# Memory's key and value projection: x's normed part and the reciprocal root in PSUM banks, and ScalarE's publication one tile later

## The chip, the cores and the metric

The kernel runs on one core of one Trainium2 chip. The metric is the device time of one launch in microseconds. Three runs of the kernel before gave 2895.95, 2902.23 and 2911.4 us; their median, 2902.23 us, is the time to beat.

## What is computed

The reference runs two blocks of two transformer layers each on x of 512 tokens by 1024 features, in float32. The change lies in the second block, in each layer's cross attention to a memory of 256 rows. Cut to that:

```
def rmsnorm(x, g):
    return x * lax.rsqrt(jnp.mean(x * x, axis=-1, keepdims=True) + EPS) * g

def second_block(x, mem, ...):
    for layer in range(2):
        y = mixer(rmsnorm(x, g_mix_pre[layer]))          # forgetting attention, then a gated recurrence
        x = x + rmsnorm(y, g_mix_post[layer])            # the x that the change touches
        h = rmsnorm(x, g_cross_pre[layer])
        m = rmsnorm(mem, g_mem[layer])
        k, v = jnp.split(m @ w_xkv[layer], 2, axis=-1)   # the key and value projection
        y = attention(h @ w_xq[layer], k, v) @ w_xo[layer]
        x = x + rmsnorm(y, g_cross_post[layer])
        ...                                              # feed forward
```

## The kernel before, in words

Everything is feature-major: x lies in SBUF as 8 parts of 128 partitions by 512 tokens, `x[:, m]`. Products of float32 are made of three matmuls (L562 to L564): a number is split into a high part in fp32r and the low rest, and TensorE adds high by high, low by high and high by low. A linear layer is a row of output tiles, each of 128 features. Tile m takes one chunk of weights, 128 x 1024, and 24 matmuls.

**The path of a chunk.** SyncE's queue loads chunk c into one of RING = 4 slots as soon as the low part of chunk c-4 is made. ScalarE makes the high part (`high`, w_hi, L1011), and waits for that slot's matmuls of chunk c-4. GpSimd makes the low part (`low`, w_lo, L484), after w_hi. TensorE's tile waits for w_lo. ScalarE stands LEAD = 3 chunks ahead: it issues w_hi of chunk m+3 at tile m.

**The stage.** `memory_attention(e)` begins with `xkv0` (and `xkv1` in the second layer): 16 tiles over memory's 256 rows, so that a matmul has 256 columns. Tiles 0 to 7 are keys (k_x), 8 to 15 are values (z_vx). VectorE evacuates each out of one of four PSUM banks (L1478); TensorE's tile m waits for the evacuation of tile m-4. Beside it the same engines finish x, since the mixer's output y_mid is still to be normed and added: after TensorE has summed the squares of y_mid (L648), `inverse_rms` makes the reciprocal root (L1454, ScalarE's root L1054, L1457) into `rstd`. Then, within VectorE's tile m for m < 8, `add_normed` multiplies y_mid by rstd in place (L1738) and adds it, times a gain, to x (L1739). ScalarE waits for that x, squares it (L1018) and makes its high part xh (L1023); that is `renormed` and `publish`. VectorE's `publish(m-1)` adds the squares up (acc, L1428) and makes the low part xl (L1435). The next layer, `xq`, multiplies xh and xl by its weights, and TensorE reads nothing of x before it.

**The order** on each engine is the program's, written out by hand. ScalarE's tile m is w_hi of chunk m+3, then `renormed(m)`. VectorE's tile m is the evacuation, L1738, L1739, then `publish(m-1)`: L1428 and L1435. ScalarE's square of part m, for m of 3 and more, waits until acc has taken in part m-2 (there are two buffers, tmpa), which is the line `act.wait_ge(acc_ready, n_.acc.n + m - 2)`.

PSUM has 8 banks. The projections use 0 to 3, bank 7 (`MISC`) holds the sums of squares, and attention uses 4 to 6 as well, at other times. `add_normed_rows` (L1759, L1763), the sister of `add_normed` behind xo and the feed forward, keeps both of these in banks already: the reciprocal root in bank 7 and the normed part in banks 4 to 6.

Of the kernel before, what the change touches and what calls it, by code (L numbers as in the profile page):

```python
# [17 lines left out]
KT = D // P  # L18
# [122 lines left out]
def two_stacks(nc, x_in, mem_in, weights, small_in, tables_in, rope_in, cmpmask_in, sel_dram, out):  # L141
    f32, f32r = mybir.dt.float32, mybir.dt.float32r
    ALU, ACT, AX = mybir.AluOpType, mybir.ActivationFunctionType, mybir.AxisListType
    ctx = ExitStack()
    with ctx:
        def sb(name, shape, dt=f32):
            return ctx.enter_context(nc.sbuf_tensor(name, shape, dt))

        def sem(name):
            return ctx.enter_context(nc.semaphore(name))  # L150


        x = sb("x", [P, KT, T])
# [5 lines left out]
        rstd = sb("rstd", [P, T])  # L159
# [28 lines left out]
        def place(name, shape, kib, dt=f32):  # L188
            if kib == 0:
                with nc.sbuf_tensor(name, shape, dt) as here:  # L190
                    return here
            with nc.sbuf_tensor(name + "_below", [P, int(kib * 256)], f32):
                with nc.sbuf_tensor(name, shape, dt) as here:
                    return here
# [53 lines left out]
        y_mid = place("y_mid", [P, KT, T], 48)  # L248
# [15 lines left out]

        ps = ctx.enter_context(nc.psum_tensor("ps", [P, 8, T], f32))
        S_BANKS, PT_BANKS, MISC = (0, 1, 2), (3, 6), 7


        w_in = [sem(f"w_in{s}") for s in range(RING)]
# [12 lines left out]
        x_ready = sem("x_ready")  # L282
# [38 lines left out]
        def gain(name, m):  # L321
            s = SMALL[f"g_{name}"].start + m
            return small[:, s:s + 1]
# [668 lines left out]
        def _(act):  # L992
            n_ = Shared()
# [26 lines left out]
            def publish(m, name):  # L1020

                square(x[:, m], m)
                A(xh[:, m], x[:, m], ACT.Copy, scale=gain(name, m)).then_inc(xh_ready, 1)  # L1023
# [28 lines left out]
            def root(n=T):  # L1052
                act.wait_ge(var_done, n_.var.next())
                A(tmpb[:, 0, 0:n], tmpb[:, 0, 0:n], ACT.Sqrt).then_inc(sd_done, 1)  # L1054

            def steps(name):
                c0 = CHUNK0[name]
                for m in range(TILES[name]):
                    if m or name not in ROWS:
                        high(c0 + m + LEAD)  # L1060
                    yield m, BANK0[name] + m
# [8 lines left out]
            def copy_values(dst, n):  # L1070
                act.wait_ge(vt_ready, n_.vt.next())
                bank = ps[:, 4 + (n_.vt.n - 1) % 4, :]
                A(dst, bank.rearrange("p (k c) -> p k c", c=dst.shape[-1]), ACT.Copy).then_inc(vt_copied, 1)
# [6 lines left out]
            def attention(steps, hooks, hi=xh):  # L1080

                s0 = n_.pairs.n
                n_.pairs.n += len(steps)
                for s in range(len(steps) + LAG):
                    slot = (s0 + s) % 4

                    def exponential(a):
                        u, n = steps[s]["two"][a], 2 * (s0 + s) + a
                        p = pr[:, n % 8, 0:u["nk"] + (u["sink"] is not None)]
                        act.wait_ge(sm_done, n + 1)  # L1090
                        A(p, p, ACT.Exp, scale=-1.0, bias=negm[:, slot, a:a + 1],  # L1091
                          accum_out=den[:, slot, a:a + 1]).then_inc(p_ready, 1)

                    def copy_turned():
                        n = 2 * (s0 + s - TURN) + 1
                        nk = steps[s - TURN]["two"][1]["nk"]
                        act.wait_ge(pt_ready, n + 1)
                        if n >= 4:
                            act.wait_ge(o_done, (n - 3) // 2)
                        A(pt[:, n % 4, 0:nk], ps[:, PT_BANKS[1], 0:nk], ACT.Copy).then_inc(pt_copied[1], 1)  # L1100

                    if s < len(steps):
                        exponential(0)
                    if TURN <= s < len(steps) + TURN:
                        copy_turned()
                    if s < len(steps):
                        exponential(1)
                    if s >= LAG and steps[s - LAG]["ends"]:
                        split_mix(steps[s - LAG]["group"], hi, s0 + s - LAG + 1)
                    for hook in hooks.get(s, []):  # L1110
                        hook()
# [158 lines left out]
            def renormed(m, name):  # L1270
                act.wait_ge(x_ready, n_.x.next())
                publish(m, name)
# [27 lines left out]
            def memory_attention(e):  # L1300
                for m, g in steps(f"xkv{e}"):
                    if m == 0:
                        root()
                    if m < KT:
                        renormed(m, f"cross_pre{e}")
                for j in range(4):
                    copy_values(v_x[:, :, j * 256:(j + 1) * 256], j)
                for m, g in steps(f"xq{e}"):
                    if m == 0:
                        root()  # L1310
                attention(UX, {})
                squares_out(f"xo{e}", y_mid)
                renormed_first(f"gu{2 + e}", f"ffn_pre{e}")
                gate_up(2 + e)
                squares_out(f"dn{2 + e}", y_dn, DN_CHUNKS)
# [93 lines left out]
        def _(dve):  # L1409
            n_ = Shared()  # L1410
            V = nc.vector
# [6 lines left out]
            def link(ins):  # L1418

                dve.wait_ge(dve_self, mark(ins))  # L1420
# [10 lines left out]
            def publish(m, name):  # L1431

                dve.wait_ge(xh_ready, n_.xh.next())
                accumulate(m)
                V.scalar_tensor_tensor(out=xl[:, m], in0=x[:, m], scalar=gain(name, m),  # L1435
                                       in1=fp(xh)[:, m], op0=ALU.mult,
                                       op1=ALU.subtract).then_inc(xl_ready, 1)
# [13 lines left out]
            def inverse_rms(dst, eps, n=T):  # L1451

                dve.wait_ge(ss_done, n_.ss.next())
                V.tensor_scalar(tmpb[:, 0, 0:n], ps[:, MISC, 0:n], 1.0 / D, eps, ALU.mult,  # L1454
                                ALU.add).then_inc(var_done, 1)
                dve.wait_ge(sd_done, n_.sd.next())
                link(V.reciprocal(dst[:, 0:n], tmpb[:, 0, 0:n]))  # L1457
# [13 lines left out]
            def tiles(name):  # L1471
                for m in range(TILES[name]):
                    dve.wait_ge(chunk_done, CHUNK0[name] + m + 1)
                    yield m, ps[:, (BANK0[name] + m) % 4, :]
# [139 lines left out]
            for m in range(17):  # L1614
                dve.wait_ge(chunk_done, in_e_chunk(m) + 1)
                bank = ps[:, (BANK0["in_e"] + m) % 4, :]
# [103 lines left out]
            def x_updated(ins):  # L1720
                ins.then_inc(x_ready, 1)
                n_.x.next()
# [10 lines left out]
            def copy_out(y):  # L1733
                return lambda m, bank: V.tensor_copy(y[:, m], bank)

            def add_normed(y, name, m):

                link(V.tensor_tensor(y[:, m], y[:, m], rstd[:], ALU.mult))  # L1738
                x_updated(V.scalar_tensor_tensor(out=x[:, m], in0=y[:, m], scalar=gain(name, m),  # L1739
                                                 in1=x[:, m], op0=ALU.mult, op1=ALU.add))  # L1740

            def copies_out(name, y, n_k=1):
# [49 lines left out]
                                           op1=ALU.subtract).then_inc(mem_ready, 1)  # L1792

            def memory_attention(e):
                for m, bank in tiles(f"xkv{e}"):
                    if m == 0:
                        inverse_rms(rstd, 1e-6)
                    scaled(k_x[:, m] if m < 8 else z_vx[:, m - 8], bank, MEM, rstd_m).then_inc(evac_done, 1)
                    if m < KT:
                        add_normed(y_mid, f"mix_post{e}", m)  # L1800
                    dve.wait_ge(evac_done, BANK0[f"xkv{e}"] + m + 1)
                    V.engine_nop().then_inc(proj_ready, 1)
                    if 1 <= m <= KT:
                        publish(m - 1, f"cross_pre{e}")
                for m, bank in tiles(f"xq{e}"):
                    if m == 0:
                        inverse_rms(rstd, 1e-6)
                    scaled(q_x[:, m], bank).then_inc(evac_done, 1)
                    dve.wait_ge(evac_done, BANK0[f"xq{e}"] + m + 1)
                    V.engine_nop().then_inc(proj_ready, 1)  # L1810
                attention(UX, {})
                copies_out(f"xo{e}", y_mid)
                inverse_rms_rows(1e-6)
                add_normed_rows(y_mid, f"cross_post{e}", f"ffn_pre{e}")
                gate_up(2 + e)
                copies_out(f"dn{2 + e}", y_dn, DN_CHUNKS)
                inverse_rms_rows(1e-6)
                add_normed_rows(y_dn, f"ffn_post{e}", None if e else "mix_pre1")
# [314 lines left out]
```

## Time and profile before

| | |
|---|---|
| median of three runs | 2902.23 us |
| profiled execution, its own time | 2906.3 us |
| its span | 2904.5 us |
| TensorE busy | 2762.4 us, 95% |
| GpSimd busy | 1280.0 us, 44% |
| ScalarE busy | 1094.4 us, 38% |
| VectorE busy | 1074.2 us, 37% |

The profiled execution took 1.8 us more than its span, and 4.1 us more than the median of the runs. The busy shares are means over the whole kernel. The stage that is changed lies twice in it: its first matmul starts at 1563.5 us in the first layer, and the same stage comes again about 762 us later. In the rows, times of start are us from the span's start.

### The profile page before, as it was taken

The numbers are of one execution on the slowest core, as the hardware profiler recorded it, in microseconds if no ns is written. First come the engines' busy times: TensorE is split into PE (matmuls) and PEld (weight loads), VectorE is DVE, ScalarE is ACT, GpSimd is POOL, SyncE is SP. The second block draws the span as 40 slices with busy tenths as digits, with TensorE's granted clock in tenths as the row PEclk, the third lists the DMA queues.
The fourth block names the chain that finished last, engine by engine and source line by source line (L and its number), as shares of the span: only waits on it lengthen the run. The fifth ranks groups of instructions, "written<-read, shape, count | busy, mean of one in ns | idle before, by whom it ended". The sixth has DMA issues, their size and how long they took to land.

```text
span 2904.5 us, 37907 instructions
## 1 busy us (share of the span) xinstructions
PE 2762.4 (95%) x13516; PEld 2255.4 (78%) x13516; DVE 1074.2 (37%) x1941; ACT 1094.4 (38%) x1777; POOL 1280.0 (44%) x715
## 2 busy tenths in 40 slices
PE   6999999999989999999998999999988889999998
PEld 5756888888857888878767887888876788788886
DVE  5675322112664222123445434221055673432212
ACT  5665323222664332232243334232236443333221
POOL 3544444444444444454324534444443363454442
PEclk9999999999999999999979999999998999999999
DMA  4301332333202223322203412323322231233331
GB/s 151 129 2 32 99 94 93 101 109 98 94 9 77 94 94 101 102 94 88 87 15 95 130 44 80 99 90 104 105 86 67 95 123 59 66 101 94 101 102 65
DMA packets 69090, 251.79 MB, mean 87 GB/s; under 512 B 7672, under 2 KB 7928, under 8 KB 68736
## 3 DMA queue, kind: packets, MB, share of 16 engines
q1 hardware_dynamic: 67104, 244.35, 26.4%
q10 hardware_dynamic: 1888, 6.14, 0.6%
q8 instruction: 61, 1.00, 0.2%
q14 instruction: 37, 0.30, 0.0%
HBM read 248.36 MB, written 2.10 MB: 86 GB/s over the span
## 4 chain that ended last, share of the span: by engine, by line
PE 88%; DVE 8%; issue 2%; ACT 2%; POOL 0%; DMA 0%; DVEq 0%; POOLq 0%; ACTq 0%
PE ps L562 26%; PE ps L563 26%; PE ps L564 26%; PE ps L700 4%; PE ps L725 3%; PE ps L711 2%; DVE acc L1428 1%; DVE xl L1435 1%; DVE pr L1528 0%; DVE y_mid L1738 0%; PE ps L670 0%; DVE ps L1759 0%; DVE r_l L1920 0%; DVE x L1739 0%; PE ps L648 0%
## 5 line engine op out<-in xcount | busy, mean ns | idle before, releaser
L484 POOL TENSOR_TENSOR w_lo<-w_raw,w_hi 128x1024 fp32r<-128x1024 f32 x462 | 1117.5, 2423 | 1357.8 <-ACT w_hi L1011 1357.5
L562 PE MATMUL ps<-xh,w_hi 128*128 128x512 f32 x2384 | 940.5, 395 | 43.6 <-DVE xl L1435 22.2
L563 PE MATMUL ps<-xl,w_hi 128*128 128x512 f32 x2384 | 933.7, 392 | 0.0
L564 PE MATMUL ps<-xh,w_lo 128*128 128x512 f32 x2384 | 933.4, 392 | 0.0
L1011 ACT ACTIVATE w_hi<-w_raw 128x1024 fp32r<-128x1024 f32 x462 | 484.4, 1053 | 548.1 <-PE ps L564 544.8
L562 PEld LDWEIGHTS ps<-xh,w_hi 128*128 128x128 f32 x2384 | 452.1, 190 | 143.6 <-issue 43.2
L563 PEld LDWEIGHTS ps<-xl,w_hi 128*128 128x128 f32 x2384 | 451.9, 190 | 94.5 <-issue 1.7
L564 PEld LDWEIGHTS ps<-xh,w_lo 128*128 128x128 f32 x2384 | 451.3, 189 | 94.6
L562 PE MATMUL ps<-hh,w_hi 128*128 128x512 f32 x704 | 273.9, 389 | 0.0
L563 PE MATMUL ps<-hl,w_hi 128*128 128x512 f32 x704 | 273.9, 389 | 0.0
L564 PE MATMUL ps<-hh,w_lo 128*128 128x512 f32 x704 | 273.9, 389 | 0.0
L1132 ACT ACTIVATE tmpa<-tmpa 128x512 f32<-128x512 f32 x88 | 55.6, 632 | 427.4 <-DVE tmpa L1478 427.3
L1478 DVE TENSOR_TENSOR tmpa<-ps,rstd 128x512 f32<-128x512 f32 x88 | 60.8, 691 | 385.6 <-PE ps L564 385.6
L1091 ACT ACTIVATE pr<-pr,negm 128x512 f32<-128x512 f32 (+2 forms) x224 | 120.0, 536 | 125.3 <-DVE negm L1528 125.1
L531 POOL TENSOR_SCALAR pr<-pr,wgt,ones 128x256 f32<-128x256 f32 (+3 forms) x160 | 91.3, 581 | 159.9 <-DVE wgt L1542 159.9
L564 PEld LDWEIGHTS ps<-hh,w_lo 128*128 128x128 f32 x704 | 132.2, 188 | 27.6
L562 PEld LDWEIGHTS ps<-hh,w_hi 128*128 128x128 f32 x704 | 132.2, 188 | 27.4
L563 PEld LDWEIGHTS ps<-hl,w_hi 128*128 128x128 f32 x704 | 132.2, 188 | 27.2
L1478 DVE TENSOR_TENSOR tmpb<-ps,rstd 128x512 f32<-128x512 f32 x96 | 66.3, 691 | 155.5 <-PE ps L564 155.4
L1588 DVE TENSOR_TENSOR x<-ps,x 128x512 f32<-128x512 f32 x32 | 22.1, 692 | 271.3 <-PE ps L564 271.3
L1528 DVE CUSTOM_DVE_ANT_0 pr<-ps,tab 128x512 f32<-128x512 f32 (+2 forms) x192 | 85.7, 477 | 85.4 <-PE ps L700 84.4
L562 PE MATMUL ps<-mem_h,w_hi 128*128 128x256 f32 x256 | 79.1, 309 | 20.3 <-POOL w_lo L484 20.3
(259 smaller groups left out, 2917.0 us busy)
## 6 DMA issues: line engine op xcount, KB each, us to landing
w_raw<-weights_in SPq DMA_DIRECT2D x462, 512.0 KB, 3.5
x<-x_in ACTq DMA_DIRECT2D x4, 512.0 KB, 10.7
mem<-mem_in ACTq DMA_DIRECT2D x2, 1024.0 KB, 4.9
x_out<-x SPq DMA_DIRECT2D x4, 512.0 KB, 2.6
rope<-rope_in ACTq DMA_DIRECT2D x1, 512.0 KB, 12.2
tab<-tables_in ACTq DMA_DIRECT2D x2, 256.0 KB, 2.9
tab<-tables_in ACTq DMA_DIRECT2D x1, 384.0 KB, 12.5
small<-small_in ACTq DMA_DIRECT2D x1, 326.5 KB, 5.4
```

The source lines that it names most:

```text
L484: nc.gpsimd.tensor_tensor(w_lo[:, slot], w_raw[:, slot], w_hi.bitcast(f32)[:, slot], ALU.subtract).then_inc(lo_ready, 1)
L531: nc.gpsimd.tensor_scalar(p, p, w, gate, ALU.mult, ALU.mult).then_inc(pn_ready, 1)
L562: nc.tensor.matmul(dst, w_hi[:, slot, w], hi, start=first, stop=False)
L563: nc.tensor.matmul(dst, w_hi[:, slot, w], lo, start=False, stop=False)
L564: return nc.tensor.matmul(dst, w_lo[:, slot, w], hi, start=False, stop=last)
L700: last = nc.tensor.matmul(ps[:, S_BANKS[n % 3], 0:u["nk"]], q, k, start=c == 0, stop=c == parts - 1)
L711: last = nc.tensor.transpose(ps[:, PT_BANKS[a], tokens(kb)], pr[:, n % 8, tokens(kb)], ident[:])
L725: last = nc.tensor.matmul(ps[rows, g["bank"], tokens(column)], values[kb], pt[:, (n + a) % 4, tokens(kb)], start=st["opens"] and kb == 0, ...
L1011: A(w_hi[:, s], w_raw[:, s], ACT.Copy).then_inc(hi_ready, 1)
L1091: A(p, p, ACT.Exp, scale=-1.0, bias=negm[:, slot, a:a + 1], accum_out=den[:, slot, a:a + 1]).then_inc(p_ready, 1)
L1478: return V.tensor_tensor(dst, bank[0:rows, 0:n], r[0:rows, 0:n], ALU.mult)
L1528: V.tensor_tensor_reduce(out=pr[:, n % 8, 0:nk], in0=ps[:, S_BANKS[n % 3], 0:nk], in1=u["mask"], scale=-u["scale"], scalar=start, op0=ALU.add,
```

## The change

It has two parts. First, VectorE writes the reciprocal root of the mixer's output into PSUM bank 6 rather than into SBUF, and the normed part of y_mid into bank 4 or 5 in turn rather than back over y_mid; L1739 reads it there. A wait keeps the bank of part m-2 until x has taken it in. Second, the publication of x's parts is moved by one tile: ScalarE does `renormed(m-1)` in tile m, for m of 1 to 8, and VectorE does `publish(m-2)` in tile m, for m of 2 to 9.

```
+        NORMED_BANKS, RSTD_BANK = (4, 5), 6
...
                 for m, g in steps(f"xkv{e}"):
                     if m == 0:
                         root()
-                    if m < KT:
-                        renormed(m, f"cross_pre{e}")
+                    if 1 <= m <= KT:
+                        renormed(m - 1, f"cross_pre{e}")
...
-            def add_normed(y, name, m):
+            def add_normed(y, name, m, x0):
 
-                link(V.tensor_tensor(y[:, m], y[:, m], rstd[:], ALU.mult))
-                x_updated(V.scalar_tensor_tensor(out=x[:, m], in0=y[:, m], scalar=gain(name, m),
+                bank = ps[:, NORMED_BANKS[m % 2], :]
+                if m >= 2:
+                    dve.wait_ge(x_ready, x0 + m - 1)
+                link(V.tensor_tensor(bank, y[:, m], ps[:, RSTD_BANK, :], ALU.mult))
+                x_updated(V.scalar_tensor_tensor(out=x[:, m], in0=bank, scalar=gain(name, m),
                                                  in1=x[:, m], op0=ALU.mult, op1=ALU.add))
...
             def memory_attention(e):
+                x0 = n_.x.n
                 for m, bank in tiles(f"xkv{e}"):
                     if m == 0:
-                        inverse_rms(rstd, 1e-6)
+                        inverse_rms(ps[:, RSTD_BANK, :], 1e-6)
                     scaled(k_x[:, m] if m < 8 else z_vx[:, m - 8], bank, MEM, rstd_m).then_inc(evac_done, 1)
                     if m < KT:
-                        add_normed(y_mid, f"mix_post{e}", m)
+                        add_normed(y_mid, f"mix_post{e}", m, x0)
                     dve.wait_ge(evac_done, BANK0[f"xkv{e}"] + m + 1)
                     V.engine_nop().then_inc(proj_ready, 1)
-                    if 1 <= m <= KT:
-                        publish(m - 1, f"cross_pre{e}")
+                    if 2 <= m <= KT + 1:
+                        publish(m - 2, f"cross_pre{e}")
```

## Rows read from the trace of the kernel before

**Rows 1.** Mean over stretches: busy us (x instructions) of PE, PEld, DVE, ACT, POOL; PEclk, DMA, GB/s.

```profile
1575.90:1612.00 36.10, 25.74 (x170) 24.98 (x169) 35.77 (x33) 17.59 (x24) 22.77 (x9) 0.82 0.33 103
...
2338.00:2374.00 36.00, 26.06 (x165) 25.38 (x165) 35.67 (x33) 17.49 (x24) 22.80 (x9) 0.81 0.33 103
```

**Rows 2.** TensorE's idle times in xkv0, from the timeline: start, us, ..., [idle before].

```profile
1578.92 0.58 PE L562 MATMUL ps<-mem_h,w_hi 128*128 128x256 f32 x1 [2.86 <-POOL w_lo L484]
...
1597.78 0.58 PE L562 MATMUL ps<-mem_h,w_hi 128*128 128x256 f32 x1 [4.27 <-POOL w_lo L484]
...
1608.04 0.39 PE L562 MATMUL ps<-mem_h,w_hi 128*128 128x256 f32 x1 [2.11 <-POOL w_lo L484]
```

**Rows 3.** GpSimd's timeline in xkv0.

```profile
1576.52 5.14 POOL L484 TENSOR_TENSOR w_lo<-w_raw,w_hi 128x1024 fp32r<-128x1024 f32 x2 [7.94 <-ACT w_hi L1011]
1584.59 5.66 POOL L484 TENSOR_TENSOR w_lo<-w_raw,w_hi 128x1024 fp32r<-128x1024 f32 x2 [2.94 <-ACT w_hi L1011]
...
1608.16 20.45 POOL L484 TENSOR_TENSOR w_lo<-w_raw,w_hi 128x1024 fp32r<-128x1024 f32 x8 [0.17 <-ACT w_hi L1011]
```

**Rows 4.** VectorE's timeline in xkv0.

```profile
1574.05 0.42 DVE L1478 TENSOR_TENSOR k_x<-ps,rstd_m 128x256 f32<-128x256 f32 x1
1574.39 0.68 DVE L1738 TENSOR_TENSOR y_mid<-y_mid,rstd 128x512 f32<-128x512 f32 x1
1575.11 0.75 DVE L1739 SCALAR_TENSOR_TENSOR x<-y_mid,small,x 128x512 f32<-128x512 f32 x1
1575.79 0.75 DVE L1435 SCALAR_TENSOR_TENSOR xl<-x,small,xh 128x512 fp32r<-128x512 f32 x1
...
1576.79 2.63 DVE L1738 TENSOR_TENSOR y_mid<-y_mid,rstd 128x512 f32<-128x512 f32 x1
1579.45 2.75 DVE L1739 SCALAR_TENSOR_TENSOR x<-y_mid,small,x 128x512 f32<-128x512 f32 x1
1582.13 0.68 DVE L1428 TENSOR_TENSOR acc<-acc,tmpa 128x512 f32<-128x512 f32 x1
1582.73 0.74 DVE L1435 SCALAR_TENSOR_TENSOR xl<-x,small,xh 128x512 fp32r<-128x512 f32 x1
1583.40 0.41 DVE L1478 TENSOR_TENSOR k_x<-ps,rstd_m 128x256 f32<-128x256 f32 x1
...
1584.44 0.75 DVE L1739 SCALAR_TENSOR_TENSOR x<-y_mid,small,x 128x512 f32<-128x512 f32 x1
1585.12 2.87 DVE L1428 TENSOR_TENSOR acc<-acc,tmpa 128x512 f32<-128x512 f32 x1
1587.91 2.88 DVE L1435 SCALAR_TENSOR_TENSOR xl<-x,small,xh 128x512 fp32r<-128x512 f32 x1
...
1616.86 1.33 DVE L1478 TENSOR_TENSOR z_vx<-ps,rstd_m 128x256 f32<-128x256 f32 x3
...
1627.11 0.42 DVE L1478 TENSOR_TENSOR z_vx<-ps,rstd_m 128x256 f32<-128x256 f32 x1 [2.45 <-PE ps L564]
```

**Rows 5.** ScalarE's timeline in xkv0.

```profile
1568.27 0.63 ACT L1054 ACTIVATE tmpb<-tmpb 128x512 f32<-128x512 f32 x1 [2.23 <-DVE tmpb L1454]
1574.16 0.63 ACT L1018 ACTIVATE acc<-x 128x512 f32<-128x512 f32 x1 [5.26 <-DVE x L1739]
1574.70 0.71 ACT L1023 ACTIVATE xh<-x,small 128x512 fp32r<-128x512 f32 x1
1575.32 1.04 ACT L1011 ACTIVATE w_hi<-w_raw 128x1024 fp32r<-128x1024 f32 x1
```

**Rows 6.** One line's instructions over the kernel: ns min/median/max, first and last start.

```profile
L1759 DVE TENSOR_TENSOR ps<-y_mid,ps x16: 680/684/697, 1758.3 to 2532.3; 128x512 f32<-128x512 f32 x16
...
L1763 DVE SCALAR_TENSOR_TENSOR x<-ps,small,x x32: 736/744/752, 1759.1 to 2900.7; 128x512 f32<-128x512 f32 x32
```

**Rows 7.** TensorE's granted clock in xkv1, in stretches of 2 us (busy us, PEclk, DMA, GB/s).

```profile
2340.00:2342.00 2.00, 1.07 (x5) 0.50 0.00 0
...
2344.00:2346.00 2.00, 2.00 (x12) 0.50 0.57 162
```

## The prediction

> **What bounds the kernel now.** I began with the shares: TensorE is busy 95% of the span, so time can only be won where it stands idle or runs slowly. In the chain of work that ended last, the longest pieces outside attention are VectorE's in the two key and value projections, so I read that stage by engine. The means over stretches show it [rows 1]: in 36.1 us of xkv0 TensorE is busy 25.7 us, at a granted clock of 0.82, and VectorE 35.8 us, all of it; xkv1 is the same (26.1, 0.81, 35.7). TensorE's idle times all end with w_lo: 2.86, 4.27, 2.11 us [rows 2]. GpSimd is no bound either, it stands 7.94 us and 2.94 us idle for ScalarE's w_hi [rows 3], and ScalarE stood 5.26 us before its first square, waiting for x [rows 5]. So VectorE sets this stage through x, ScalarE's order carries that to w_hi, then w_lo, then TensorE.
>
> The reader is to see next why VectorE is slow. The same instruction takes 0.68 or 2.63 us (L1738), 0.75 or 2.75 (L1739), 0.68 or 2.87 (L1428), 0.75 or 2.88 (L1435) [rows 4]. The long ones fall where GpSimd makes w_lo, and end with it: a pair of w_lo lasts 1584.59 to 1590.25 [rows 3]; L1428 begins at 1585.12, the first w_lo ends at about 1587.42 (half), and L1435 starts at 1587.91. The instructions that are stretched read two tensors from SBUF. L1478 reads one from PSUM and one from SBUF, and three of them take 1.33 us together at 1616.86, in the middle of eight w_lo in a row [rows 3, 4]. So an instruction with two SBUF inputs and a w_lo exclude each other.
>
> **Rules for a schedule, from rows.** Start to start on VectorE, free of w_lo [rows 4]: L1478 0.34 us, L1738 0.72, L1739 0.67, L1428 0.62, L1435 0.67. An instruction with two SBUF inputs that meets a w_lo lets the next one start 0.48 us after that w_lo's end, and the w_lo behind it ends 2.83 us after the last one's end (5.66 for two); a free w_lo is 2.39 us (5.14 for a pair that VectorE entered once, less 2.75) [rows 3]. ScalarE: square 0.54, xh 0.62, w_hi 1.04, then w_lo may start 0.16 later (1575.32 + 1.04 + 0.16 = 1576.52) [rows 3, 5]. A tile of TensorE is 2.88 us at full clock, the distance of the last evacuations (2.45 idle + 0.42) [rows 4]. A gap of about 2 us or more brings the granted clock down to 0.50 for some us; a mean of 0.82 over 36.1 us [rows 1] is 13 us of it for three gaps, part of that still idle, so I take 3 us at half speed, 1.4 us of delay, for each. I worked the order of before through with these rules: it gives the last L1478 at 1627.0, the trace 1627.11 [rows 4].
>
> **Part 1, the banks.** Of VectorE's four instructions per part that can be shut out, two no longer can be: L1738 and L1739 now have one SBUF input. Nothing is added but a wait for VectorE's own x of two parts earlier, long done. Cost of the operands: the sister lines write and read PSUM alike at 684 and 744 ns [rows 6], against 0.68 and 0.75 [rows 4]: nothing, at most 0.03 us an instruction either way, 16 a stage, 0.5 us. The reciprocal now writes a bank; no row has that, I take the time of before, the bound is the same 0.5 us either way.
>
> The Trainium skill, "VectorE: DVE Perf Modes", section on the TRN2 errata, gives 62 cycles more for a PSUM source than for SBUF; by it the 16 instructions would cost an estimated 1.0 us a stage more. This trace does not agree: 744 against 750 ns [rows 4, 6].
>
> **Part 2, the order.** It takes w_hi of chunk 4 out from behind x of part 0. The root ends at 1568.90 [rows 5], so w_hi 4 ends at 1569.9 and w_lo 4 at 1572.5, under VectorE's reciprocal (which has one input): tile 4 starts at 1575.9 without the gap of 2.86 [rows 2]. Every later w_hi moves one part ahead likewise. What it costs: ScalarE's square of part j waits until acc holds part j-2. That sum stood in VectorE's tile j-1, before x of j, and now stands in tile j, behind it. So the sum, which w_lo can shut out, comes into the chain that feeds w_hi j+5. Queued behind the waiting square are xh, the next w_hi, and through it w_lo and TensorE. No DMA is issued by ScalarE here. Loads follow w_lo, they come earlier or as before, and SyncE's queue has only them.
>
> **The schedule after, xkv0** (x_j is the end of L1739):
>
> - x0 1574.05, x1 1575.8, x2 1577.5 (in before behind two w_lo). xl0 meets w_lo 5 (to 1578.9): next at 1579.35. x3 1581.1. acc1 behind w_lo 6 (1581.7), xl1 behind w_lo 7 (1584.5): 1585.0. x4 1586.7.
> - acc2 behind w_lo 8 (1587.3): 1587.8. Now square 4 (waited 1.1 us for it), xh, w_hi 9 end at 1590.05, w_lo 9 from 1590.2 to 1593.15. xl2 goes free, x5 1590.2, acc3 free, xl3 behind w_lo 9: 1593.6. x6 1595.4. acc4 behind w_lo 10 (1596.0), xl4 free, x7 1598.8. From x5 to x7 two parts take 8.65 us; before they took 10.3 (TensorE's restarts at 1597.78 and 1608.04 [rows 2]).
> - acc5 free, xl5 behind w_lo 11 (1601.8): 1602.3. ScalarE has no more x to wait for, so w_lo runs without a pause, and acc6, xl6, acc7, xl7 are each behind one: 1605.1, 1607.9, 1610.7, 1613.5. Evacuations 8, 9, 10 stand among them and end at 1602.6, 1608.25, 1613.9.
> - TensorE: no gap until tile 9, which waits 2.8 us for w_lo 9; tile 11 1.5 us for w_lo 11; tile 13 0.7 us for evacuation 9; tile 14 2.7 us for evacuation 10. From 1613.9 two tiles, 5.76, and 1.4 us for the clock: 1621.1; the last L1478 1621.1 against 1627.0 in the schedule of before.
>
> That is 5.9 us a stage; the projection of q behind it is TensorE's, so it keeps them. Two stages: 11.8, say 12. The span goes from 2904.5 to 2892.5, the profiled execution from 2906.3 to 2894.3. Its own time was 4.1 us over the median of the runs; against 2902.2 the forecast is 2890.2.
>
> **Bounds.** (a) acc3 would start at 1590.17 and w_lo 9 at 1590.21: a tie. Rows have VectorE 0.15 us first and winning (L1739 at 1584.44, w_lo at 1584.59), and w_lo 0.27 us first and winning (1576.52, L1738 at 1576.79) [rows 3, 4], none between. I let the earlier go first. If w_lo 9 alone wins, it and w_hi 10's chain turn out earlier and the stage ends at 1620.1: 1.0 us more gain. (b) The clock: nothing for it after the last gap gives 1619.7, or 1.4 more gain; low for 6 us instead of 3 takes 1.4 of gain. (c) Latencies of 0.1 us more or less in a semaphore move the end by 0.5. Together 4 to 8 us a stage, 8 to 16 for both, 2886 to 2894; the median of a few runs moves by some 4 us more.
>
> The Trainium skill, "SBUF — State Buffer", section "Who interferes with whom", says that whichever of the two starts first holds the shared pair for its whole instruction. On the tie it sides with the schedule (5.9 us a stage) against (a)'s 6.9; the rows ahead agree with it as far as they reach.
>
> **Rivals.**
>
> 1. *The acc wait doesn't bind*, the gain of part 1 comes whole. Part 1 with the order of before, where the sum stands ahead of x, gives by the same rules an end at 1618.8: 8.2 us a stage, 16.4 in all, 2885.8. For it: square 4 waits but 1.1 us, and a tie the other way takes most of that off. Against: L1428 is shut out in every second part. Chance 0.27.
>
> 2. *w_lo gets in ahead of acc in every part.* Then from x_j: w_lo 2.35, acc 0.48 behind, square to w_hi 2.27, and 0.16, so the next w_lo at 5.26; VectorE meanwhile acc 2.83, xl 0.66, evacuation and x 1.73, 5.22: a cycle that keeps itself, 5.2 a part, no better than before's 5.13. Three such parts from x4 make x7 1602.4, the end 3.6 later: 2.3 us a stage, 4.6 in all, 2897.6. For it: these two numbers are so near. Against: it needs GpSimd ahead each time by a few hundredths. Chance 0.08.
>
> 3. *Slower: the clock stays low.* The gaps move from tiles 4, 6, 8, 10 to 9, 11 and 14, the last just ahead of q's projection, whose matmuls are twice as long. Low clock still stood at 0.50 some 3 to 5 us after a restart in xkv1 [rows 7]. If from the restart at 1593.2 it stayed low, seven tiles of twice 2.88 us end at 1633.5, 6.5 later than before, and two tiles of q's, with twice the columns, take 11.5 us more: 18 us a stage, 2902.2 + 36 = 2938. It decides from 12 us of low clock a stage beyond the schedule's 3 (each costs half). Against: in both stages clock came back within some 6 us. Chance 0.04.
>
> That the change does nothing, as the freed time turns up as longer acc and xl, is 2 at its limit; 0.02.
>
> **How the numbers follow.** The forecast, between 8 and 14.5 us of gain, has 0.59, rival 1 0.27, rival 2 0.08, rival 3 0.04, nothing 0.02. 0.5% is 14.5 us, about what a measurement can tell from no change. Faster by more than that: most of rival 1 and a little of the forecast that the scatter of a median carries over, 0.28. Slower by more: rival 3, 0.04. Within: 0.68. The range takes in rival 1 and the scatter below, rival 2 in part above: 2881 to 2898.
>
> **What would show it.** L1738 and L1739 never over 0.8 us; L1428 and L1435 still up to 2.9, in xkv0 about 11 of 15; x2 at 1577.5, the last L1478 near 1621 instead of 1627.1; no gap before tile 4, gaps ahead of tiles 9, 11, 14; a square that waits for acc. Wrong would make it: L1739 stretched although it has one SBUF input, x ready but ScalarE waiting for something else, or a clock under 0.8 in the stretch after 1612.

## The result and the profile after

| | before | after |
|---|---|---|
| median of seven runs, us | 2895.95 (2888.23 to 2911.4) | 2880.88 (2877.97 to 2886.92) |
| profiled span, us | 2904.5 | 2880.3 |
| first to last evacuation of xkv0, us | 54.79 | 49.17 |
| first to last evacuation of xkv1, us | 54.81 | 47.67 |

The ratio is 0.9943, with a 95% interval of 0.9921 to 0.9966: 16.5 us faster by the median ratio, 10 to 23 by the interval. Repeated later with 12 runs it was 0.9956 (0.9936 to 0.9976), 12.7 us. The change made the kernel faster. The measured time, 2880.88 us, lies 0.12 us outside the range of 2881 to 2898; the repeat's median, 2880.45 us, lies outside it too.

The profiled spans lie 24.2 us apart. Only 12.8 of that is the two stages (54.79 - 49.17 = 5.62, 54.81 - 47.67 = 7.14); 13.5 us are already there when the first evacuation starts, at 1558.8 against 1572.3 us, and the rest of the kernel gives 2.1 us back. An experiment below shows what the 13.5 us are.

VectorE's timeline in xkv0 of the kernel after:

```profile
1558.81 0.42 DVE L1479 TENSOR_TENSOR k_x<-ps,rstd_m 128x256 f32<-128x256 f32 x1
...
1566.23 0.68 DVE L1742 TENSOR_TENSOR ps<-y_mid,ps 128x512 f32<-128x512 f32 x1
1566.94 0.75 DVE L1743 SCALAR_TENSOR_TENSOR x<-ps,small,x 128x512 f32<-128x512 f32 x1
1567.62 1.18 DVE L1429 TENSOR_TENSOR acc<-acc,tmpa 128x512 f32<-128x512 f32 x1
1568.72 2.90 DVE L1436 SCALAR_TENSOR_TENSOR xl<-x,small,xh 128x512 fp32r<-128x512 f32 x1
...
1584.66 0.75 DVE L1743 SCALAR_TENSOR_TENSOR x<-ps,small,x 128x512 f32<-128x512 f32 x1
...
1588.70 0.41 DVE L1479 TENSOR_TENSOR z_vx<-ps,rstd_m 128x256 f32<-128x256 f32 x1
1589.23 2.35 DVE L1429 TENSOR_TENSOR acc<-acc,tmpa 128x512 f32<-128x512 f32 x1
1591.50 2.89 DVE L1436 SCALAR_TENSOR_TENSOR xl<-x,small,xh 128x512 fp32r<-128x512 f32 x1
...
1599.91 1.80 DVE L1479 TENSOR_TENSOR z_vx<-ps,rstd_m 128x256 f32<-128x256 f32 x4
...
1607.98 0.42 DVE L1479 TENSOR_TENSOR z_vx<-ps,rstd_m 128x256 f32<-128x256 f32 x1 [2.65 <-PE ps L565]
```

GpSimd's, of the same stretch:

```profile
1563.01 8.07 POOL L485 TENSOR_TENSOR w_lo<-w_raw,w_hi 128x1024 fp32r<-128x1024 f32 x3 [4.12 <-ACT w_hi L1012]
...
1576.89 2.77 POOL L485 TENSOR_TENSOR w_lo<-w_raw,w_hi 128x1024 fp32r<-128x1024 f32 x1 [2.99 <-ACT w_hi L1012]
```

The two instructions that went to banks, 1566.23 and 1566.94, run in 0.68 and 0.75 us in the middle of three w_lo in a row. Before, their like took 2.63 and 2.75 us at such a place [rows 4]. The two that still have two SBUF inputs are still shut out, up to 2.90 us: 11 of the 15 such instructions in xkv0, as the prediction said.

ScalarE's timeline, and TensorE's idle times:

```profile
1555.29 1.04 ACT L1012 ACTIVATE w_hi<-w_raw 128x1024 fp32r<-128x1024 f32 x1
...
1574.54 0.63 ACT L1019 ACTIVATE tmpa<-x 128x512 f32<-128x512 f32 x1 [3.45 <-DVE acc L1429]
```

```profile
1579.71 0.39 PE L563 MATMUL ps<-mem_h,w_hi 128*128 128x256 f32 x1 [2.45 <-POOL w_lo L485]
...
1588.28 0.58 PE L563 MATMUL ps<-mem_h,w_hi 128*128 128x256 f32 x1 [2.56 <-POOL w_lo L485]
...
1600.45 0.38 PE L563 MATMUL ps<-mem_h,w_hi 128*128 128x256 f32 x1 [1.84 <-DVE z_vx L1479]
```

The w_hi of chunk 4 follows the root at once. The gap ahead of tile 4 [rows 2] is gone; gaps stand ahead of tiles 9, 11 and 14, and sum to 6.9 us against 10.4 before (the three of [rows 2], and one of 1.12 us ahead of tile 6 that the prediction passed over). A square now ends its wait with acc (1574.54), where before it ended with x.

### The profile page after: what moved, and what is told of

Its sections match the earlier page's. It is cut to its first block, busy times and chain, and to the rows that moved or that the text cites. A ratio compares the mean times of both kernels' runs of the same rounds, so it can differ in the third digit from the quotient of the medians.

```text
span 2880.3 us, 37907 instructions
## 1 busy us (share of the span) xinstructions
PE 2746.6 (95%) x13516; PEld 2241.9 (78%) x13516; DVE 1064.4 (37%) x1941; ACT 1093.5 (38%) x1777; POOL 1281.3 (44%) x715
## 4 chain that ended last, share of the span: by engine, by line
PE 88%; DVE 8%; issue 2%; ACT 2%; DMA 0%; POOL 0%; DVEq 0%; POOLq 0%; ACTq 0%
PE ps L563 26%; PE ps L565 25%; PE ps L564 25%; PE ps L701 4%; PE ps L726 3%; PE ps L712 2%; DVE xl L1436 1%; DVE acc L1429 1%; DVE pr L1529 0%; PE ps L671 0%; DVE ps L1763 0%; DVE r_l L1925 0%; DVE tmpb L1922 0%; DVE ps L1742 0%; PE ps L649 0%
## 5 line engine op out<-in xcount | busy, mean ns | idle before, releaser
L1479 DVE TENSOR_TENSOR tmpa<-ps,rstd 128x512 f32<-128x512 f32 x88 | 60.8, 691 | 385.6 <-PE ps L565 385.6
L1568 DVE TENSOR_TENSOR hl<-tmpb,hh 128x512 f32 (+1 forms) x88 | 63.8, 725 | 79.6 <-ACT hh L1137 79.6
(260 smaller groups left out, 2890.2 us busy)
```

Of the source, the lines that this page charges most:

```text
L1479: return V.tensor_tensor(dst, bank[0:rows, 0:n], r[0:rows, 0:n], ALU.mult)
L1568: V.tensor_tensor(at(hl), tmpb[:, j % 2], at(fp(hh)), ALU.subtract).then_inc(hl_ready, 1)
```

## The experiments

The measure that tells versions apart best is the distance from the first to the last evacuation (k_x to z_vx) of each stage: it repeats within 0.1 us where the clock does not interfere, while whole runs of one kernel scatter by 30 us. The schedule of the prediction was continued with each edit and its figure put down before the run.

| version | schedule, us | xkv0 | xkv1 | ratio to before (95%) |
|---|---|---|---|---|
| before | 54.7 | 54.79 | 54.81 | |
| after | 48.8 | 49.17 | 47.67 | 0.9943 (0.9921 to 0.9966) |
| after, again | 48.8 | 47.65 | 47.69 | 0.9956 (0.9936 to 0.9976) |
| e1, banks alone | 46.5 | 46.98 | 46.99 | 0.9929 (0.9902 to 0.9957) |
| e2, order alone | 52.0 | 52.42 | 52.39 | 0.9987 (0.9960 to 1.0014) |
| e3, banks, only ScalarE later | 43.6 | 44.14 | 44.14 | 0.9913 (0.9886 to 0.9941) |
| e4, after, acc in a bank | 42.4 | 42.15 | 42.15 | 0.9907 (0.9873 to 0.9942) |
| e5, e3, acc in a bank | 41.3 | 40.83 | 40.84 | 0.9905 (0.9873 to 0.9938) |
| e6, only ScalarE later, no banks | 55.3 | 54.04 | 55.50 | 0.9984 (0.9965 to 1.0003) |

**a_same**, the kernel before against itself, no edit.

> The kernel before, unchanged, timed against itself: what two equal kernels show apart, and whether the stretch ahead of the changed stage moves by itself. The profile after gained 13 us between 1443.7 us (start of the forgetting attention) and the changed stage, where both kernels run the same instructions, at a mean clock of 0.69 before and above 0.9 after. Theory 1 (chance of one execution): the ratio here is 1.000 within 0.003, and this profile may show either level of clock there. Theory 2 (the change itself does it): this profile shows the low clock of before again, with the evacuations of the two key and value stages 54.8 us from first to last in either case.

The ratio was 0.9997 (0.9970 to 1.0023), the stages 54.77 and 54.81 us. Its twelve runs go from 2884.24 to 2917.43 us. Its profile had the low clock in the forgetting attention again, which this run alone could not tell from theory 2.

**b_after**, the kernel after again, no edit.

> The kernel after, unchanged, again. The two stages account for 12.8 us of the 24.2 between the profiled spans; 13.5 us lay ahead of the first, in the forgetting attention, whose length also moved in other runs (60.9 us in two executions of the kernel before, 48.2 to 52.1 in four of others). Theory 1: ratio 0.9943 to 0.9960 (12.8 us is 0.44%), stages at 49.2 and 47.7 us again within 1.5. Theory 2 (the change shortens the attention ahead of it as well): ratio near 0.990.

It settles that. Stretches of 10 us of the forgetting attention (busy us, PEclk, DMA, GB/s), first of this execution, then of the first profile of the kernel after:

```profile
1450.00:1460.00 10.00, 10.00 (x42) 0.50 0.00 0
1460.00:1470.00 10.00, 10.00 (x42) 0.50 0.00 0
...
1490.00:1500.00 10.00, 10.00 (x45) 0.50 0.00 1
```

```profile
1450.00:1460.00 10.00, 9.43 (x34) 0.58 0.00 0
1460.00:1470.00 10.00, 9.42 (x82) 1.00 0.00 0
```

The same kernel, the same instructions: once the granted clock is at 1.2 GHz for over 50 us there, once it is back at 2.4 GHz by 1460 us. The attention took 70.0 us in this execution and 48.2 in the other, the span was 2899.0 against 2880.3 us. Yet the ratio of the runs is 0.9956, what the stages alone give: the repeat's 7.14 + 7.12 = 14.3 us is 0.49%, the first profile's 12.8 is 0.44%; theory 2's 0.990 lies outside the interval. Over ten profiles of eight kernels this stretch took from 48.1 to 72.3 us. The two kernels before took 60.8 and 60.9 us for it. Theory 2 fell: of the 13.5 us ahead of the stage, 12.6 are this attention's (60.8 less 48.2), a chance of one execution.

**e1_banks.** Part 1 alone: in the kernel after,

```
-                    if 1 <= m <= KT:
-                        renormed(m - 1, f"cross_pre{e}")
+                    if m < KT:
+                        renormed(m, f"cross_pre{e}")
...
-                    if 2 <= m <= KT + 1:
-                        publish(m - 2, f"cross_pre{e}")
+                    if 1 <= m <= KT:
+                        publish(m - 1, f"cross_pre{e}")
```

> Part 1 alone: the banks, with the publication order of before. By the schedule of the prediction the last evacuation comes 46.5 us after the first instead of 54.8 (8.2 us less a stage, 16.4 in all), TensorE keeps its gap before tile 4, and ScalarE's squares never wait for acc. That would be more than both parts together (5.9 a stage forecast, 5.6 and 7.1 measured): the order takes some back. Rival: the order carries the gain, and part 1 alone gives less than both, under 5 us a stage.

46.98 us: 7.8 less than before, where both parts together gave 5.6 to 7.1. The banks are the gain, and the order as it was changed takes some of it back: 0.7 us in three of the four stages of the kernel after, 2.2 in the one whose last gap was followed by the low clock. TensorE keeps its gap ahead of tile 4, 2.88 us. ScalarE's squares end their waits with x, not with acc:

```profile
1567.92 0.63 ACT L1019 ACTIVATE tmpa<-x 128x512 f32<-128x512 f32 x1 [3.47 <-DVE x L1743]
...
1571.40 0.63 ACT L1019 ACTIVATE tmpa<-x 128x512 f32<-128x512 f32 x1 [1.28 <-DVE x L1743]
```

**e2_order.** Part 2 alone: the kernel before, with `renormed(m - 1)` for m of 1 to 8 and `publish(m - 2)` for m of 2 to 9.

> Part 2 alone: the publication one tile later on both engines, root and normed part in SBUF as before. By the schedule 2.7 us less a stage, 5.4 in all, with L1738 and L1739 still stretched to 2.6 and 2.8 us. Rival: the later order is what freed the stage, then 5 us or more a stage.

52.4 us, 2.4 less a stage: the rival, 5 us or more, fell. The ratio cannot be told from 1. VectorE's timeline still has the long ones:

```profile
1566.07 2.79 DVE L1739 SCALAR_TENSOR_TENSOR x<-y_mid,small,x 128x512 f32<-128x512 f32 x1
1568.79 2.89 DVE L1435 SCALAR_TENSOR_TENSOR xl<-x,small,xh 128x512 fp32r<-128x512 f32 x1
1571.60 0.41 DVE L1478 TENSOR_TENSOR k_x<-ps,rstd_m 128x256 f32<-128x256 f32 x1
1571.93 2.55 DVE L1738 TENSOR_TENSOR y_mid<-y_mid,rstd 128x512 f32<-128x512 f32 x1
```

**e3_scalar_late.** The kernel after, with VectorE's publication moved back:

```
-                    if 2 <= m <= KT + 1:
-                        publish(m - 2, f"cross_pre{e}")
+                    if 1 <= m <= KT:
+                        publish(m - 1, f"cross_pre{e}")
```

> The kernel after with only VectorE's publish moved back to publish(m-1) in tile m for m of 1 to 8; ScalarE stays one tile later. Now the sum of part j-2 stands ahead of x of part j again, and w_hi of chunk 4 still does not wait for x of part 0. By the schedule 11.1 us less a stage than before, 22 in all, some 5 us a stage less than the kernel after; no square waits for acc. Rival (the acc wait costs nothing): equal to the kernel after within 1 us a stage.

44.14 us in both stages, 5.0 less than after's first and 3.5 less than its others. The rival fell: beside the banks it is VectorE's half of part 2 that costs, the half that the title does not name. The acc sum stands ahead of x again, so the square waits only for x:

```profile
1570.82 0.63 ACT L1019 ACTIVATE tmpa<-x 128x512 f32<-128x512 f32 x1 [3.53 <-DVE x L1743]
...
1578.53 0.63 ACT L1019 ACTIVATE tmpa<-x 128x512 f32<-128x512 f32 x1 [2.03 <-DVE x L1743]
```

**e6_scalar_late_only.** The kernel before, with ScalarE's half of part 2 and nothing else.

> The kernel before, with only ScalarE's publication one tile later (VectorE's publish as before, no banks). w_hi of chunk 4 comes 6 us earlier and the gap ahead of tile 4 goes. By the schedule the stage gains nothing (55.3 us from first to last evacuation against 54.8): VectorE's own chain sets the end, and a gap of TensorE that lies ahead is worth nothing. Rival (the gap of 2.9 us and the low clock behind it are worth their length): 3 us or more less a stage.

54.04 and 55.50 us: no gain that both stages show, and the rival, 3 us or more, fell, though the gap ahead of tile 4 is gone; TensorE's first one comes later:

```profile
1596.73 0.39 PE L562 MATMUL ps<-mem_h,w_hi 128*128 128x256 f32 x1 [2.55 <-POOL w_lo L484]
```

VectorE's chain set the end, so a gap of TensorE's that lies before it was worth nothing by itself. The 1.5 us between the two stages are the clock's: both have a last gap of 1.85 us, ahead of tile 14. Up to it the two stages run alike (45.12 and 45.10 us from the first evacuation). Behind it the granted clock stayed at 1.00 in xkv0 and fell in xkv1:

```profile
1628.00:1630.00 2.00, 2.00 (x19) 1.00 0.43 115
...
2390.00:2392.00 2.00, 2.00 (x11) 0.50 0.29 76
```

What a half of part 2 is worth depends on the banks. ScalarE's half gains 2.8 us a stage once they have shortened VectorE's chain (e1 to e3, 46.98 to 44.14). VectorE's half, put on top of ScalarE's, gains 1.6 and 3.1 us without the banks (e6 to e2, 54.04 and 55.50 to 52.4) and costs 3.5 to 5.0 with them (e3 to after). No run has VectorE's half alone, and none takes apart why its sign turns.

**e4_acc_bank.** The kernel after, and acc of this stage in bank 7 until its last addition:

```
-                return A(acc[:, 0:n] if m == 0 else tmpa[:, m % 2, 0:n], src, ACT.Square)
+                return A((ps[:, MISC, 0:n] if in_bank else acc[:, 0:n]) if m == 0 else tmpa[:, m % 2, 0:n], src,
+                         ACT.Square)
...
-                V.tensor_tensor(acc[:, 0:n], acc[:, 0:n], tmpa[:, m % 2, 0:n], ALU.add).then_inc(acc_ready, 1)
+                src = ps[:, MISC, 0:n] if in_bank else acc[:, 0:n]
+                V.tensor_tensor(acc[:, 0:n] if m == KT - 1 else src, src, tmpa[:, m % 2, 0:n],
+                                ALU.add).then_inc(acc_ready, 1)
```

> The kernel after, and acc of this stage lies in bank 7 until its last addition, so that the sum has one SBUF input. If the exclusion by w_lo of instructions with two SBUF inputs is the whole mechanism, L1428's successors take 0.69 us each but the last, the squares' wait for acc costs 0.8 us at most, and the stage from first to last evacuation is 42.4 us by the schedule, 6.8 less than after's 49.2. Rival (the order itself, not the exclusion of acc, takes the time): over 47 us.

42.15 us, against 42.4 of the schedule; the rival, over 47, fell. Of the additions even the last, into SBUF but out of a bank, is 0.69 us long, while the xl around it are still shut out. Seven w_lo follow one another meanwhile:

```profile
1598.07 0.70 DVE L1431 TENSOR_TENSOR ps<-ps,tmpa 128x512 f32<-128x512 f32 x1
1598.68 1.99 DVE L1439 SCALAR_TENSOR_TENSOR xl<-x,small,xh 128x512 fp32r<-128x512 f32 x1
1600.60 0.41 DVE L1482 TENSOR_TENSOR z_vx<-ps,rstd_m 128x256 f32<-128x256 f32 x1
1601.12 0.69 DVE L1431 TENSOR_TENSOR acc<-ps,tmpa 128x512 f32<-128x512 f32 x1
```

```profile
1597.72 17.46 POOL L485 TENSOR_TENSOR w_lo<-w_raw,w_hi 128x1024 fp32r<-128x1024 f32 x7 [0.64 <-ACT w_hi L1012]
```

It is the inputs that count, not the output, and the rule is not special to the two instructions of the change.

**e5_acc_bank_scalar_late.** The same edit on e3.

> The same acc bank on the version in which only ScalarE is one tile later. By the schedule 41.3 us a stage, against 44.1 measured without the acc bank: the sum is off ScalarE's path there already, so what is left is the length of VectorE's last parts. 16 tiles of 2.88 us from the first matmul, with 0.9 for the sum of squares, set 38.2 us as the floor of this distance (first evacuation 8.8 us after the first matmul). If xl alone now keeps the stage, the acc bank gives 1 us or less.

40.83 and 40.84 us, 3.3 less a stage than e3: more than the 1 us of its last sentence, and 0.5 less than the schedule. It is the shortest stage of all, 14.0 us under before and 2.6 over the floor of 38.2. By the runs e3, e4 and e5 cannot be told apart (0.9913, 0.9907, 0.9905); the stages say 21.3, 25.3 and 27.9 us. Their medians, 2872.05, 2868.17 and 2871.74 us, lie 8 to 13 us under the kernel after's 2880.88 and 2880.45. Only of e3 does every run (2869.34 to 2875.33) lie under all nineteen of the kernel after (the fastest 2877.76).

## Why the prediction was right and where it was wrong

**The mechanism was right, to tenths of a microsecond.** The exclusion of w_lo and instructions with two SBUF inputs, and the order of the waits, carry the whole stage. Moved by the 13.51 us by which this execution was ahead (1572.32 less 1558.81), the trace against the schedule: the instruction next after x of part 2 starts at 1577.5 (schedule 1577.5), evacuation 4 starts at 1585.06 (1585.0), that of tile 8 at 1602.2 (1602.3), that of tile 10 at 1613.4 (1613.5), the last at 1621.5 (1621.1). L1742 and L1743 are never over 0.75 us. TensorE's gaps came at tiles 9, 11 and 14, as said; their lengths, 2.45, 2.56 and 1.84, were 2.8, 1.5 and 2.7 in the schedule, with 0.7 at tile 13 that did not appear. They differ because the schedule put low clock behind the gap ahead of tile 9 and none behind the one ahead of tile 11, and it was the other way round; w_lo of chunk 11 and the evacuations, which end these gaps, came when the schedule had them.

**Rule and price.** The operands in PSUM cost nothing, 0.68 and 0.75 us as before; the 1.0 us a stage estimated from the Trainium skill ("VectorE: DVE Perf Modes", section on the TRN2 errata) isn't seen here either. The reciprocal into bank 6 takes 3.36 us, in SBUF the line takes 3.35 in the same kernels, so the bound of 0.5 us for it was not needed. In the tie, (a), VectorE's L1429 began 0.13 us ahead of w_lo (1576.76 against 1576.89) and went first in 0.69 us, as the schedule had it. The Trainium skill, "SBUF — State Buffer", section "Who interferes with whom", gives the shared pair to whichever starts first, and this row agrees.

**The clock, (b), gave a part of what was over.** In xkv0 the last gap was followed by low clock, in xkv1 not:

```profile
1602.00:1604.00 2.00, 2.00 (x11) 0.50 0.43 119
1604.00:1606.00 2.00, 2.00 (x15) 0.69 0.78 242
...
2350.00:2363.60 13.60, 11.30 (x93) 10.89 (x91) 8.94 (x10) 3.88 (x4) 13.30 (x6) 1.00 0.62 192
```

The stages are 49.17 and 47.67 us, 1.5 apart, where I had 1.4 for it. Both stages of the repeat are as the faster one: the term was right in size where the clock fell, and in three of four stages it did not. With it the stage gained 5.6 us against 5.9 forecast, without it 7.1 against 7.3. The rule it came from, that a gap of about 2 us or more brings the clock down, did not hold (see the last section). So the gain is 5.6 to 7.1 a stage and 12.8 to 14.3 in all, where I had 11.8: a term of the sum off by 1.0 to 2.5 us.

**What failed is the level, and with it the range.** The step is "against 2902.2 the forecast is 2890.2". 2902.23 was the median of three runs, and of seven it was 2895.95; over the runs of the experiments the kernel before had medians of 2895.5, 2896.3 and 2893.7. That is 6 us, half of the forecast gain. From 2895.95 the same gain ends at 2884.2 with 11.8, and at 2881.7 with 14.3, against 2880.88 measured. I allowed 4 us for the scatter of a median, with three runs that were 15 us apart. Put about 2895.95, the same range is 2875 to 2892 and holds the measured time. The scatter goes with the granted clock: of the 23 runs of the kernel before that stand beside b_after, those of 2885 to 2888 us had a mean clock of 0.979 or 0.980, those of 2903 to 2911 us 0.969 to 0.972. Where in a run the low clock lies, only a profile shows. In the two profiles of the kernel after, whose spans are 18.7 us apart, the forgetting attention is 21.8 us apart; that it makes the scatter of the other runs too is likely and not shown. The trace of the kernel before had a mean clock of 0.69 there (1440 to 1512 us), and I did not look. The remaining us between the stages' 12.8 to 14.3 and the ratio's 16.5 lie inside its interval, and the repeat's 12.7 lies on the other side.

**The rivals.** Rival 1, the whole gain of part 1, is not what happened, yet its price was right as a price: e1 gave 7.8 us a stage where it had 8.2. By size alone the stages of 7.1 us would fit it nearly as well as the forecast; what speaks against it is that squares did wait for acc in the kernel after, and e3. Rival 2, w_lo ahead of acc every time, did not occur: three acc in after, at 1573.27, 1576.76 and 1581.86, were 1.17, 0.69 and 1.17 us long, none 2.8. Rival 3, the low clock that stays, did not occur in the stage. It does exist in this kernel, but in the forgetting attention, in both kernels alike. The 0.5% bound fell between the two measurements (0.57% and 0.44%), so that "within" at 0.68 was fair but "faster" at 0.28 rather low.

What stays open is why the clock in the forgetting attention comes back after 10 us in one execution and after more than 50 in another of the same kernel. No run here was made for it.

## What to carry to other kernels

When a row's longest time is four times its shortest, look for what another engine does just then: here VectorE's instructions with two SBUF inputs and GpSimd's low parts exclude each other, and one input moved to a PSUM bank freed an instruction at no cost. Moving a step later on one engine also moves whatever it hands back, so ask of each engine on its own whether it gains, and ask anew after every other change: beside the banks ScalarE's half of the move was worth 2.8 us a stage and VectorE's cost 3.5 to 5.0, without them VectorE's gained 1.6 to 3.1. And before a gain of 0.4% is forecast as an absolute time, ask how far the runs of the kernel before lie apart.

## What the runs showed of the hardware that was not expected

- How long TensorE had paused did not tell whether its clock came down. The kernel before had kept 1.00 (2.4 GHz) behind a gap of 1.12 us and fallen to 0.50 (1.2 GHz) behind those of 2.11 us and more. In the four stages of the kernel after (two in each of its two profiles) it stayed at 1.00 behind 2.42 to 2.45 us ahead of tile 9 each time, fell behind 2.55 to 2.56 us ahead of tile 11 each time, and fell behind the 1.78 to 1.84 us ahead of tile 14 once. In e6 the same 1.85 us ahead of tile 14 did it in one stage and not in the other. Of xkv0 in the kernel after:

```profile
1580.00:1582.00 2.00, 2.00 (x19) 1.00 0.55 166
...
1588.00:1590.00 2.00, 1.72 (x8) 0.54 0.31 61
```

- The granted clock in one and the same attention stretch stayed at 0.50 for anything from some 10 to over 60 us, and moved that stretch from 48.1 to 72.3 us over ten profiles: more than the whole change is worth.
